# Nine stage edges of a two-block transformer kernel: loads in pieces, first products regrouped, gates finished one stage earlier

## The reference, cut to what matters

```python
def _gated_readout(o, og, gain):
    return _merge(_rms(o, gain) * jax.nn.silu(og))
...
    q = _heads(jax.nn.silu(fq), HGRN_HEADS)
    i = _heads(fi, HGRN_HEADS)
    og = _heads(fog, HGRN_HEADS)
...
    o_lat = _gated_readout(dirs[0][1] + dirs[1][1], og[:, :, n_ctx:], out_norm)
```

```python
    affinity = jax.nn.softmax((h @ router_w).astype(F32), axis=-1)
    gate, idx = lax.top_k(jnp.swapaxes(affinity, 1, 2), cap)
    xe = jax.vmap(lambda hb, ib: hb[ib])(h, idx)
    hid = jax.nn.silu(jnp.einsum('becd,edf->becf', xe, w_gate)) * jnp.einsum('becd,edf->becf', xe, w_up)
```

## Time and profile before

| | us |
|---|---|
| median of 3 runs (4405.62 to 4419.54) | 4415.44 |
| profiled execution | 4411.0 |
| its span | 4409.2 |
| TensorE busy | 4042.8 (92%) |
| VectorE busy | 1666.8 (38%) |
| ScalarE busy | 881.9 (20%) |
| GpSimd busy | 743.6 (17%) |

### The profile page before, as it was taken

The page is one execution under the profiler, slowest core; times in us unless marked ns, Lnnn a source line. Parts: engine busy times, 40 slices in busy tenths (PEclk is TensorE's granted clock), DMA queues, the critical chain, the costliest instruction groups (busy, mean ns, idle before and its releaser), DMA issues. The chain is left out here.

```text
span 4409.2 us, 46565 instructions
## 1 busy us (share of the span) xinstructions
PE 4042.8 (92%) x18631; PEld 2449.3 (56%) x18631; DVE 1666.8 (38%) x2942; ACT 881.9 (20%) x1666; POOL 743.6 (17%) x505
## 2 busy tenths in 40 slices
PE   7997889999989998899988999989998897999988
PEld 4664445554446765588546777775554445433433
DVE  2346342225724453433555566550024223111111
ACT  3124320000122333200013333321022211000000
POOL 0003212223411111123323333320002200000000
PEclk8999999999999999999999999999998997999999
DMA  4117511114421101353441000004200223899998
GB/s 167 39 43 261 169 40 64 64 43 148 170 84 29 53 29 59 117 209 116 144 117 29 22 27 20 17 32 142 70 1 1 108 84 126 361 421 421 422 421 369
DMA packets 317021, 579.68 MB, mean 131 GB/s; under 512 B 55836, under 2 KB 186108, under 8 KB 316168
## 3 DMA queue, kind: packets, MB, share of 16 engines
q1 hardware_dynamic: 316808, 576.70, 35.4%
HBM read 566.02 MB, written 10.63 MB: 131 GB/s over the span
## 5 line engine op out<-in xcount | busy, mean ns | idle before, releaser
L2951 PE MATMUL dn_ps<-room,dn_w 128*128 128x512 f32 (+1 forms) x616 | 226.1, 520 | 4.8 <-DVE dn_qx L3470 2.5
L764 PE MATMUL ffn_up_ps<-room,ffn_up_w 128*128 128x384 f32 (+1 forms) x704 | 209.0, 441 | 12.4 <-DMA ffn_up_w<-in_ffn_w_gate 12.4
L764 PE MATMUL ffn_up_ps<-ffn_up_t,room 128*128 128x384 f32 (+1 forms) x704 | 205.7, 436 | 0.8 <-DVE room L844 0.8
L764 PE MATMUL ffn_up_ps<-room 128*128 128x384 f32 (+1 forms) x704 | 203.9, 432 | 0.0
L4478 PE MATMUL experts_ps<-experts_ring,experts_xs 128*64 128x512 f32 (+1 forms) x768 | 165.3, 582 | 27.8 <-DMA experts_ring<-in_w_up 27.8
L2374 PE MATMUL hgrn_ps<-room,hgrn_w 128*128 128x512 f32 x384 | 175.2, 597 | 0.0
L764 PEld LDWEIGHTS ffn_up_ps<-room,ffn_up_w 128*128 128x128 f32 x704 | 135.2, 193 | 71.7 <-DMA ffn_up_w<-in_ffn_w_gate 13.2
L4478 PE MATMUL experts_ps<-experts_ring,room 128*64 128x512 f32 (+1 forms) x768 | 160.7, 570 | 8.7 <-DMA experts_ring<-in_w_up 8.1
L2951 PEld LDWEIGHTS dn_ps<-room,dn_w 128*128 128x128 f32 x616 | 116.3, 194 | 94.2 <-issue 81.7
L764 PEld LDWEIGHTS ffn_up_ps<-ffn_up_t,room 128*128 128x128 f32 x704 | 134.8, 192 | 57.6 <-DVE room L844 1.7
L4511 PE MATMUL experts_ps<-experts_ring,experts_hidT 128*64 128x512 f32 x704 | 155.0, 594 | 11.6 <-issue 6.9
(11 more groups left out here) (626 smaller groups left out, 7204.5 us busy)
## 6 DMA issues: line engine op xcount, KB each, us to landing
experts_ring<-in_w_gate SPq DMA_DIRECT2D x128, 704.0 KB, 15.8
experts_ring<-in_w_up SPq DMA_DIRECT2D x128, 704.0 KB, 17.8
experts_ring<-in_w_down SPq DMA_DIRECT2D x160, 512.0 KB, 14.5
ffn_down_w<-in_ffn_w_down SPq DMA_DIRECT2D x55, 1024.0 KB, 4.7
att_wm<-in_mod_w SPq DMA_DIRECT2D x20, 2048.0 KB, 8.9
ffn_up_wm<-in_ada_w SPq DMA_DIRECT2D x12, 2048.0 KB, 12.3
ffn_up_w<-in_ffn_w_up SPq DMA_DIRECT2D x22, 1024.0 KB, 7.7
ffn_up_w<-in_ffn_w_gate SPq DMA_DIRECT2D x20, 1024.0 KB, 5.3
```

The source lines that it names most:

```text
L764: mm = nc.tensor.matmul(result(n, p), lhs[:, k, :], rhs[:, k, :], start=k == 0, stop=k == half - 1)
L2951: mm = nc.tensor.matmul(out, ahead.tile[:, k, :] if k < by_ahead else wt[:, h % 2, piece, k, :], hT[:, k, tok], start=k == 0, stop=k == KD ...
```

## The change

Seven edits, each at the start or the end of a phase:

1. `opening`: the last modulation block is loaded in four DMAs of two feature slices each, with a semaphore each, and TensorE waits for them one by one.
2. `closing` with `ahead` (`out0` and `wo`): the products whose weights lie in `first` are issued for all tiles first, then the others tile by tile.
3. `down`: for the last two tiles, VectorE's steps are interleaved, and the gate multiplication of the one is put before the mean of the other.
4. `odd_mixer`: head 0's projections come before the values' first block. `first` holds their first two slices (three DMAs of 128 columns), and the first quarters of q, forward and backward gate are issued together.
5. `odd_mixer` and `closing`: the gates leave PSUM through Silu, and GpSimd multiplies them by the gain, unit by unit, behind head 7's other work; `closing` no longer does either.
6. `route`: the ranks come from four matmuls, of 64, 48, 32 and 16 columns.
7. `route` and `experts`: `route` writes `pick` only for the first four experts; VectorE writes the other twelve experts' part at the start of `experts`, behind its wait for the gate vector.

```diff
@@ opening
+                    for n, (k0, k1) in enumerate(PIECES_OF_LAST):
+                        sp.dma_start(wt[:, b, k0:k1, :], mod.w[:, k0:k1, bass.ts(mod.b0 + b, 512)]).then_inc(S["last_in"][n], 16)
@@ closing
+            if ahead:
+                wd = jobs[0][2]
+                pe.wait_ge(ahead.sem, 16)
+                for i, t in enumerate(tiles):
+                    for k in range(n_ahead):
+                        nc.tensor.matmul(ps[:, i, 0:wd], xT[:, k, t * P:(t + 1) * P], ahead.tile[:, k, 0:wd], start=k == 0, stop=False)
...
-                    for k in range(kt):
+                    for k in range(0 if j else n_ahead, kt):
...
-                nc.scalar.activation(gates_o[:, i, :], gates_o[:, i, :], ACT.Silu).then_inc(S["o_silu"], 1)
...
-                dve.wait_ge(S["o_gate"], i + 1)
...
-                    nc.gpsimd.tensor_tensor(gate, gate, gain_h[:, :].unsqueeze(1).broadcast_to([P, heads, P]), ALU.mult).then_inc(S["o_gate"], 1)
@@ down
+            one, other = finished_beside(n_pairs)
+            mean_y(one)
+            gated(one)
+            mean_y(other)
+            residual(one)
+            gated(other)
+            mean_x(one)
+            residual(other)
+            normed(one)
+            mean_x(other)
+            normed(other)
@@ odd_mixer
+        if h + 1 < H:
+            project(h + 1)
         if h == -1:
             tokens("v", 0, 0)
-        if h + 1 < H:
-            project(h + 1)
...
+            together = [(u, 0) for u in range(3)]
+            return {0: together + [uq for uq in quarters if uq not in together]}
...
+                    k0 = 0 if j else n_ahead
                     for piece in range(3):
-                        sp.dma_start(wt[:, s, :, piece * P:(piece + 1) * P], heads_v[piece, n]).then_inc(S["w_in"][s], 16)
+                        sp.dma_start(wt[:, s, k0:, piece * P:(piece + 1) * P], heads_v[piece, n][:, k0:, :]).then_inc(S["w_in"][s], 16)
...
+                        nc.scalar.activation(dst, ps[:, bank, 0:b - a], ACT.Silu).then_inc(S["evac"], 1)
...
+            for u in gate_units:
+                what, n, j, t = units[u]
+                a, b = vcuts[n]
+                pool.wait_ge(S["evac"], evac_through[u])
+                gate = gate_out[:, t - CTX_TILES, a:b].rearrange("p (h f) -> p h f", f=P)
+                nc.gpsimd.tensor_tensor(gate, gate, gain.unsqueeze(1).broadcast_to([P, (b - a) // P, P]), ALU.mult).then_inc(S["gate_done"], 1)
@@ route
-            for m in range(tiles):
-                for before in range(m + 1):
-                    mm = nc.tensor.matmul(ps[:, 3, m * E:(m + 1) * E], cst[:, UPTO[0], :] if before == m else ones, taken[:, before, :],
-                                          start=before == 0, stop=before == m)
+            for later in range(tiles):
+                mm = nc.tensor.matmul(ps[:, 3, later * E:tiles * E], ones if later else cst[:, UPTO[0], :], flat[:, 0:(tiles - later) * E], start=later == 0, stop=later == tiles - 1)
...
+                picks(nc, pick, slot, slot_iota, m, 0, GROUP)
@@ experts
+                        if of == 1 and i == 0:
+                            pe.wait_ge(S["picked"], tiles)
...
+            for m in range(tiles):
+                picks(nc, pick, slot, slot_iota, m, GROUP, EXPERTS).then_inc(S["picked"], 1)
```

More of the change, by code:

```diff
@@ L1216, in _ @@
                 collect(p)
-            last = finished_beside(n_pairs)
-            for t in last:
-                mean_y(t)
-            for t in last:
-                residual(t)
-            for t in last:
-                mean_x(t)
-                normed(t)
-            for t in last:
-                take(n_pairs, t)
+            one, other = finished_beside(n_pairs)
[9 more added lines that the diff above has]
+            normed(other)
+            take(n_pairs, one)
+            take(n_pairs, other)
 LEVELS = 7
@@ L2199, with odd_mixer @@
 HGRN_HEADS = 8
-def odd_mixer(nc, tag, hT, w_in, bounds, o, sets, spare, cst, ident, ahead):
+def odd_mixer(nc, tag, hT, w_in, bounds, o, sets, spare, cst, ident, ahead, out_gain, gain):
     H, N = HGRN_HEADS, N_TOK
@@ L2341, in odd_mixer, with weights @@
             arrived.append(per_slot[j % ring])
+        def weights(j, k):
+            return ahead.tile[:, k, :] if j == 0 and k < n_ahead else wt[:, j % ring, k, :]
+        gate_units = [u for u, unit in enumerate(units) if unit[0] == "gate"]
         @block.tensor
@@ L4264, in route @@
         taken = sb("taken", tiles, E)
-        slot = sb("slot", tiles, E)
         ps = stack.enter_context(nc.psum_tensor(f"{tag}_ps", [P, 8, 512], F32))
```

96 lines of the change are left out of this document (54 added, 42 removed).

## The result

| | before | after |
|---|---|---|
| median, us | 4415.29 (4405.62 to 4419.54) | 4358.17 (4355.05 to 4363.84) |
| profiled execution | 4411.0 | 4358.8 |
| its span | 4409.2 | 4357.0 |
| mean granted TensorE clock | 0.959 | 0.964 |

The ratio is 0.9875, 95% interval 0.9856 to 0.9894: 1.25% faster. Forecast were 4366.6 us (range 4352 to 4384) and a gain of 48.8 us; the two profiles differ by 52.2 us. A second series on another chip gave 4360.27 against 4408.23, a gain of 48.0, and a third 4362.05 against 4409.96, a gain of 47.9.

The account below looks back on a forecast made before the run. TensorE, busy 92% of the span, was taken as the bound: matmuls plus pauses between phases and the clock after them. Terms summed to 48.8 us; 4411.0 became 4362.2, plus 4.4 gave 4366.6 us, range 4352 to 4384.

Parts of the forecast that it names:

- opening: Last modulation block in four pieces: only a quarter of its products follows the last landing, 2.4 us saved, bounds 0 to 2.5.
- `wo` (with the merge): Start of `wo`: early-weight products for four tiles remove pauses of 1.31 and 0.99 and slow restarts, 2.9 us saved.
- `down`, both: End of both `down` phases: reordered VectorE steps end each about 1.2 us earlier, 2.4 together.
- gates in head 7: Head 7 of `odd_mixer`: twelve added GpSimd multiplications, 9.3 us, are covered by VectorE's waits; cost 0, upper bound 9.3.
- the 4.4 that I added: Whole kernel: 4.4 us, by which the median before lay above its profiled execution, added to 4362.2 to give 4366.6.
- nothing more is gained: `out1`, first tile: transposes start 9.4 us earlier, but the restart stays as slow, half clock being granted from 1738 on.
- both move together: `route` and experts: TensorE releases the weight stream, so the gather's 5.8 us earlier start is kept to the end.
- rival (a): Experts: bytes over rate set the weight stream's end, so the 5.8 us are missing, 4372.4 us; chance 0.07.
- (b): `odd_mixer`: head 0's weights come late, pause and half clock stay, 4.6 us less gain, 4371.2 us; chance 0.13.
- (c): Head 7: GpSimd's products delay it and TensorE by at most 9.3 us, 4375.9 us; chance 0.07.
- (d): `out0` and `wo`: clock falls for another reason and weights land later, about half of 13.1 missing, 4373.2 us; chance 0.06.
- (e): Projections and feed-forward: denser TensorE work draws half clock, kernel slower than before, 4426.6 us at 120 us of it; chance 0.03.

Follow-up runs that it names:

- A second series: The changed kernel again with no edit, the source of its second profile: 4360.27 us, before 4408.23; ratio 0.989.
- a third: The changed kernel once more, unedited, beside the two kernels with filled waits, the source of its third profile: 4362.05 us, before 4409.96; ratio 0.9887.
- the three other series: Changed kernel unedited, 4360.27 us; changed kernel with old ranks and whole selection in `route`, 4366.05 us; changed kernel unedited beside the filled-wait kernels, 4362.05 us.

## Why the prediction was right, point by point

All terms are within 1.9 us of what they measured, each read off its own phase. "Undone" is the kernel that undoes this edit against the changed one.

| step | forecast | after against before | undone |
|---|---|---|---|
| opening | 2.4 | 2.7 | 1.3 |
| `out0` | 10.2 | 10.1 | 8.4 |
| `wo` (with the merge) | 2.9 | 2.3 | 2.9 |
| `down`, both | 2.4 | 2.1 (waits: 2.3) | 2.6 |
| `odd_mixer` | 11.4 | 11.8 | 13.0 |
| `out1` | 13.7 | 12.7 | 12.5 |
| gates in head 7 | 0 | 0 | 0 |
| `route` and experts | 5.8 | 4.5 | 4.3 |
| sum | 48.8 | 46.2 | 45.0 |

(`down` undone is read from its two waits.) The other 6.0 us of the 52.2 lie in phases that no edit touches (latent attention 3.6, delta mixer 2.1, second up projection 1.8, linear recurrence ahead of the attention 0.9, attention -2.4). In four of the five the granted clock goes with it: its cost there fell by 4.5, 2.0 and 1.9 us in the first three and rose by 2.3 in the attention; in the recurrence it rose by 0.8, and its 0.9 us stay open. The third profile of the same kernel has a span of 4362.0, a gain of 47.2 and not of 52.2.

The forecast time is 8.4 us above the measured median. Of that, 3.4 are the gain by profiles, 52.2 instead of 48.8: the terms together were 2.6 too high, and the untouched phases gave 6.0. Of these, the latent attention and the attention move by as much between profiles of one kernel (364.5 and 367.7; 199.2 to 204.3), which is chance. The delta mixer and the second up projection don't; values like those of before stand only in single kernels with another edit (706.33; 300.4 to 301.2), so whether the change moved these two for good, by 3.9 us, stays open. The other 5 are the 4.4 that I added because the median of before lay higher than its profiled execution, and the 0.7 by which the median of after lies below its own. The 4.4 belonged to these few runs: the three other series have the kernel before at 4408.2, 4406.6 and 4410.0, and against the first and third of them the gain is 48.0 and 47.9. So the size of the sum was right by its own steps; that it matches these two gains within 1 us is in part luck, since terms that are off by up to 1.9 and the clock cancel.

The steps that were mis-sized:

- **`out1`, "nothing more is gained" from the clock.** The restart was even slower. These are the windows of the first eight product records, before and after:

```profile
1751.52:1756.80 5.28, 5.28 (x10) 2.39 (x11) 3.85 (x5) 1.30 (x2) 0.00 (x0) 0.69 0.01 3
1717.51:1723.88 6.37, 6.37 (x10) 2.79 (x11) 3.85 (x5) 0.21 (x1) 0.00 (x0) 0.57 1.05 387
```

The eight took 5.28 us at a granted clock of 0.69 before, and 6.37 at 0.57 after. The half clock began inside the wait in both (at 1737.7 and at 1712.7) and ended at 1754.8 and 1722.9, so behind the shorter wait more of it fell on the products, 5.4 us instead of 3.2. That is the 1 us that is missing.

- **`route`, "both move together".** 5.76 us came at the experts' first matmul as forecast. Behind it 1.5 were given back against the kernel undone, 1.0 in the gather's half clock and 0.5 in the wait for expert weights (1.12 instead of 0.66), and 1.1 against before, 0.5 and 0.7 (0.43 there). In the second and third profile of the same kernel these first waits sum to 0.94 and 1.65. Only this part, 0.5 to 0.7 us, is what rival (a) said.
- **`wo`.** Behind the pause at the phase's start, 1.44 to 1.75 us, half clock was granted in 4 of 12 profiles with the new order. I had counted only pauses that the edit removes.
- **`down`.** The waits fell by 1.32 and 0.97 (before had 9.59 in the second, the old order has it at 9.95 here); by the undone order it is 1.3 each, where I took 1.2. The missing 0.35 in the second goes with the early gates: it has 8.27 where they are undone and 8.62 in the other kernels with the new order. No run shows why.
- **Gates in head 7.** The twelve products took 10.9 us on GpSimd and not 9.3, and VectorE's waits for the copy there were seven before, 24.5 us in sum and up to 4.6 long, where I had read five and 3.7 for one in each step: the term of 0 held, with more room than I had read.
- **Opening.** A quarter took 0.62 and not 0.83, and the full block 1.93 or 3.30: the term is 1.3 to 2.7 by the clock, and less when the last piece is late.

The rivals: (b) fails by a margin of 1 us, the weights land 5.8 us after the first matmul and the work ready lasts 6.9; at full clock it lasts 5.2 and TensorE waits 0.41 to 0.43. (a) fails but for the 0.5 to 0.7 above. (c) fails, even four times the work isn't seen. (d) fails in `out0`, whose length is the same in all twelve profiles with the new order. (e), more half clock in a denser stream, fails: the clock's cost did not rise (124.8 us before, 109.1 to 124.1 over the thirteen profiles of the changed kernel and its variants; outside of the experts 111.7 and 91.9 to 107.9).

## What to carry to other kernels

Count an edge as its pause plus the half clock behind it. In these runs the second part went where TensorE had work through most of the wait; where what is ready can be put ahead (products for all tiles, first quarters together), both go. Look for an engine's waits before you count the price of work beside it: head 7 took 10.9 us of GpSimd's products, and 40 more, for nothing. Compare edits of a few microseconds phase by phase between matmul ends; the total of one and the same kernel moved by 9 us from execution to execution (4355.05 to 4363.84).

## What the runs showed of the hardware that was not expected

- The clock fell inside a wait, not at its end. In the second profile of the changed kernel, TensorE's last product of the first `down` ends at 1220.98 and its wait lasts to 1229.25; the windows (columns as above) have the clock third from the end:

```profile
1224.00:1225.00 1.00, 0.00 (x0) 0.00 (x0) 0.96 (x3) 0.20 (x1) 0.00 (x0) 1.00 0.00 0
1225.00:1226.00 1.00, 0.00 (x0) 0.00 (x0) 1.00 (x2) 0.49 (x1) 0.00 (x0) 0.59 0.00 0
1226.00:1227.00 1.00, 0.00 (x0) 0.00 (x0) 0.88 (x4) 0.78 (x3) 0.00 (x0) 0.50 0.00 0
```

- The same instructions came with few discrete lengths over the changed kernels: the latent attention 364.4 to 364.6 (seven profiles) or 367.5 to 367.8 (six), `wo`'s start 7.11 (eight) or 8.80 (four) and the merge ahead of it the complement, so that their sum stays at 193.3 to 193.8. There, a stretch of half clock that one phase missed was met by the next.
- Pieces of 512 KB behind three blocks of 2 MB were there when the 2 MB block was (34.82 to 34.98 against 34.97) in nine profiles, and once at 36.37.
- In the experts, where TensorE also waits for weights, 11.2 us of half clock's cost instead of 16.8 left the length the same (672.2 and 672.0 us, one program).
